# Experts in units of 64 tokens, two neighbouring units per step, each expert's weights loaded once in fixed order

## The reference

```
g_top, g_idx = lax.top_k(softmax(t @ w_grp + b_grp), 1)          # 1 of 4 groups
e_sel = the 4 logits of that group out of t @ w_rtr + b_rtr
e_top, e_idx = lax.top_k(softmax(e_sel), 2)                      # 2 of its 4 experts
expert_id = g_idx * 4 + e_idx                                    # 16 experts
weights = g_top * e_top / sum(e_top)
a = einsum('td,edf->tef', t, w_gate); u = einsum('td,edf->tef', t, w_up)   # d 1024, f 256
hid = silu(a) * u * gates
y = einsum('tef,efd->td', hid, w_down)
```

```
layer 0  pairs 314 152 100 198 7 13 11 7 89 88 30 33 85 45 55 53
         tiles   3   2   1   2 1  1  1 1  1  1  1  1  1  1  1  1   = 20
         units   5   3   2   4 1  1  1 1  2  2  1  1  2  1  1  1   = 29, 15 steps of two units
layer 1  pairs 204  88 198 114 19 34 33 54 38 34 14 42 77 152 55 124
         tiles   2   1   2   1  1  1  1  1  1  1  1  1  1   2  1   1   = 19
         units   4   2   4   2  1  1  1  1  1  1  1  1  2   3  1   2   = 28, 14 steps of two units
```

```
layer 0  0-0 0-0 0-1 1-1 2-2 3-3 3-3 4-5 6-7 8-8 9-9 10-11 12-12 13-14 15
layer 1  0-0 0-0 1-1 2-2 2-2 3-3 4-5 6-7 8-9 10-11 12-12 13-13 13-14 15-15
```

## Time and profile before

| what | value |
| --- | --- |
| median of 3 runs | 1613.76 us (1613.31 to 1620.27) |
| the profiled execution | 1615.13 us |
| its span, first to last instruction | 1613.4 us |
| mean granted TensorE clock | 0.928 |
| PE busy | 1388.2 us |
| gate/up products of L1903 | 279.9 us busy, 624 instructions |
| down products of L1926 | 140.5 us busy, 312 instructions |
| expert stage of layer 0, first gate/up to last down | 548.7 to 784.7 us |
| expert stage of layer 1 | 1333.9 to 1557.5 us |

### The profile page before, as it was taken

The page is one execution under the profiler, slowest core; times in us unless marked ns, Lnnn a source line. Parts: engine busy times, 40 slices in busy tenths (PEclk is TensorE's granted clock), DMA queues, the critical chain, the costliest instruction groups (busy, mean ns, idle before and its releaser), DMA issues.

```text
span 1613.4 us, 22451 instructions
## 1 busy us (share of the span) xinstructions
PE 1388.2 (86%) x8194; PEld 840.4 (52%) x8194; DVE 728.6 (45%) x1673; ACT 434.2 (27%) x991; POOL 245.3 (15%) x374
## 2 busy tenths in 40 slices
PE   4999978999998699999479997799999939999950
PEld 3455455777676454545144554477776724454420
DVE  0345325767544334343345442377764343343426
ACT  2111146666301011111121103466660101111112
POOL 3311020000200122111302001100011010111114
PEclk8899989999998799999789997899999959999985
DMA  9500694001305699999560034800111029999943
GB/s 333 188 12 1 246 372 102 1 1 41 118 40 183 233 356 356 386 372 359 181 224 12 1 106 168 250 2 2 40 51 42 27 82 352 367 370 368 369 161 146
DMA packets 152035, 283.17 MB, mean 176 GB/s; under 512 B 7312, under 2 KB 95632, under 8 KB 146928
## 3 DMA queue, kind: packets, MB, share of 16 engines
q1 hardware_dynamic: 126832, 197.41, 36.5%
q0 software_dynamic: 25088, 84.24, 14.0%
HBM read 244.43 MB, written 37.29 MB: 175 GB/s over the span
## 4 chain that ended last, share of the span: by engine, by line
PE 50%; DVE 8%; DMA 5%; DVEq 2%; issue 2%; ACT 1%; POOL 0%; SPq 0%; POOLq 0%; ACTq 0%
PE ps L1903 16%; PE ps L1926 7%; PE ps L1642 7%; PE ps L1540 6%; PE ps L1818 4%; PE ps L1698 3%; PE ps L1751 2%; DMA ring<-in_w_mod 2%; DMA ring<-in_moe_w_up 1%; DVE ring L1221 1%; DVE x L1059 1%; DVEq L1053 1%; PE ps L1558 1%; PE ps L1874 1%; PE ps L1840 1%
## 5 line engine op out<-in xcount | busy, mean ns | idle before, releaser
L1903 PE MATMUL ps<-ring,hT_region 128*128 128x512 f32 x624 | 279.9, 602 | 2.6 <-DVE hT_region L1482 1.7
L1642 PE MATMUL ps<-ring,hT_region 128*128 128x512 f32 (+1 forms) x640 | 270.6, 579 | 1.7 <-ACT hT_region L848 1.7
L1221 DVE TENSOR_SCALAR_CACHE_REDUCE ring<-ps 128x768 f32<-128x768 f32 (+1 forms) x168 | 132.7, 820 | 164.8 <-PE ps L1698 108.4
L1642 PEld LDWEIGHTS ps<-ring,hT_region 128*128 128x128 f32 x640 | 121.2, 193 | 133.5 <-issue 132.7
L1903 PEld LDWEIGHTS ps<-ring,hT_region 128*128 128x128 f32 x624 | 117.6, 194 | 137.9 <-issue 137.0
L907 ACT ACTIVATE ring<-ring,negm 128x768 f32<-128x768 f32 (+1 forms) x168 | 137.7, 820 | 33.3 <-DVE ring L1221 33.2
L1818 PE MATMUL ps<-ring,hT_region 128*128 128x384 f32 (+1 forms) x480 | 141.8, 453 | 0.0
L1926 PE MATMUL ps<-arena,work 128*128 128x512 f32 x312 | 140.5, 593 | 1.1 <-DVE work L1505 1.1
L1698 PE MATMUL ps<-arena,qT 64*128 64x384 f32 (+1 forms) x640 | 127.5, 517 | 13.2 <-DVE ring L1221 5.7
L1489 DVE TENSOR_SCALAR work<-work 128x256 f32<-128x256 f32 x39 | 11.5, 294 | 263.2 <-ACT work L995 263.2
L1818 PEld LDWEIGHTS ps<-ring,hT_region 128*128 128x128 f32 x480 | 89.8, 190 | 44.2 <-issue 0.7
(11 more groups left out here) (270 smaller groups left out, 1612.0 us busy)
## 6 DMA issues: line engine op xcount, KB each, us to landing
ring<-in_w_mod SPq DMA_DIRECT2D x24, 2048.0 KB, 12.1
ring<-in_moe_w_gate SPq DMA_DIRECT2D x39, 1024.0 KB, 11.9
ring<-in_moe_w_up SPq DMA_DIRECT2D x39, 1024.0 KB, 15.4
arena<-in_moe_w_down SPq DMA_DIRECT2D x39, 1024.0 KB, 7.9
y_rows<-arena POOLq DMA_DIRECT2D x39, 512.0 KB, 7.7
ring<-in_w_in SPq DMA_DIRECT2D x6, 2048.0 KB, 18.9
y_rows<-x POOLq DMA_DIRECT2D x1, 7680.0 KB, 25.9
arena<-mod_rows POOLq DMA_DIRECT2D x14, 512.0 KB, 6.2
```

The lines of the kernel that those rows point to most:

```text
L1221: ts(o_, i_, -pair_of(p)[4], None, ALU.mult, ALU.min, accum_out=col).then_inc(m_ready, 1)
L1642: last = mm(ps[:, b, 0:n], hT[:, c, t * P:(t + 1) * P], w[:, c, :], start=(c == 0), stop=(c == KC - 1))
L1903: last = mm(ps[:, 2 + i % 2, :], hgT[i % 2][:, c, :], w[:, c, :], start=(c == 0), stop=(c == KC - 1))
```

## The change

The slots of an expert are now counted in units of 64 instead of tiles of 128, with at least one unit for each expert (k64[0] is -1). A step takes two neighbouring units, 128 slots as before. If both belong to one expert, the products are as before. If they belong to two, each product is issued as two, with 64 columns of the stationary operand each: the odd expert's slots are the first half and write PSUM partitions 0 to 63, the even expert's write 64 to 127. N_ET falls from 25 to 18. The DVE works out, for each step, which form it has (EI_FORM), in which ring slot the first operand lies (EI_A), and for each unit its expert, its slot and whether its expert is new (EI_NEW); PE and SP read these into registers and branch on them. PE's operand addresses in ring and arena now come from a register.

Each expert's weights are loaded once, in the order 0 to 15, expert e into the slot LATE[e % 4], gate/up in the ring and down in four arena buffers instead of two. Experts 0 to 3 are loaded without waiting for the routing, each as its ring slot comes free, the down weights once the output projection is done. An expert from 4 on is loaded when its first unit comes up: gate/up for step i when gate_up(i - 2) is done, down for step i - 1 when down(i - 3) is done.

On PE gate_up(i) now goes ahead of hidden_T(i - 1), and on DVE the copy of the rows of tile i + 1 ahead of hidden(i). The new tables are made on DVE behind r_hot and ahead of the copy of idx; the gate weights rout_w move behind it. Some constants and buffers move, and a 256-byte table is loaded at the start.

```diff
+HALF = P // 2
+N_ET = ((N_PAIR + NE * HALF) // HALF - 1 + 1) // 2
...
+LATE = (3, 2, 0, 1)
+EVEN_SLOTS = (LATE[0], LATE[2])
...
-        uses += [("moe", l, i, late[i % RING]) for i in range(N_ET)]
+        uses += [("moe", l, e, LATE[e]) for e in range(RING)]
...
+            def gate_up_of_step(l, i):
+                sp.wait_ge(gu_done[l], i - 1)
+                for u in (2 * i, 2 * i + 1):
+                    with first_of_expert(u):
+                        e, at = expert_and_slot(l, u)
+                        gate_up_weights(l, e, ring[:, bass.ds(sp.snap(at * 4096), 4096)], wgu_landed[l][u % RING])
+                    with sp.Else():
+                        sp.sem_inc(wgu_landed[l][u % RING], 32)
+            def down_of_step(l, i):
+                sp.wait_ge(dn_done[l], i - 1)
...
                 if kind == "moe":
+                    slot_free(g)
+                    gate_up_weights(l, l * NE + i, to, wgu_first[i])
+                    if i == 0:
+                        sp.wait_ge(wo_done, l * 15 + 15)
+                    down_weights(l, l * NE + i, arena[:, DN0 + 2048 * at:DN0 + 2048 * (at + 1)], wd_first[i])
+                    if i == RING - 1:
+                        sp.wait_ge(experts_ready, l + 1)
+                        for step in range(2, N_ET + 1):
+                            if step < N_ET:
+                                gate_up_of_step(l, step)
+                            if step > 2:
+                                down_of_step(l, step - 1)
...
+                tt(r_le.rearrange("p (e s) -> p e s", e=NE), lane[:, 0:NE].unsqueeze(2).to_broadcast([P, NE, NE]),
+                   lane[:, 0:NE].unsqueeze(1).to_broadcast([P, NE, NE]), ALU.is_ge)
                 dve.wait_ge(r_count, l + 1)
...
-                tt(b6, r_incl[0:1, :].unsqueeze(1).to_broadcast([1, N_ET, NE]),
-                   iota_t[0:1, :].unsqueeze(2).to_broadcast([1, N_ET, NE]), ALU.is_le)
-                red(r_ex[0:1, :], b6, AX.X, ALU.add)
+                ts(r_par, r_incl[:, 0:NE:2], 0.5, None, ALU.mult)
+                tt(b7, r_par.unsqueeze(2).to_broadcast([P, NE // 2, N_ET + 1]),
+                   halves.unsqueeze(1).to_broadcast([P, NE // 2, N_ET + 1]), ALU.is_equal)
+                red(r_par, b7, AX.X, ALU.add)
+                tt(v3(r_add, NE), v3(r_rank, NE), r_lim.unsqueeze(1).to_broadcast([P, NT, NE]), ALU.is_ge)
...
                 last.then_inc(r_hot, 1)
+                tt(b6, r_incl[row, :].unsqueeze(1).to_broadcast([1, N_HALF, NE]),
+                   iota_t[row, :].unsqueeze(2).to_broadcast([1, N_HALF, NE]), ALU.is_le)
+                red(r_ex[row, :], b6, AX.X, ALU.add)
+                for k in range(2):
+                    dve.drain()
+                    tt(b9, b8, by_step[row, k, :].unsqueeze(1).to_broadcast([1, N_ET, 2 * NE]), ALU.mult)
+                    dve.drain()
+                    red(r_steps[row, k * N_ET:(k + 1) * N_ET], b9, AX.X, ALU.add)
+                tt(b6, b6, slot_step[row, :].unsqueeze(1).to_broadcast([1, N_HALF, NE]), ALU.mult)
+                red(r_at[row, :], b6, AX.X, ALU.add)
...
+                stt(experts_i[row, EI_NEW + 1:EI_NEW + N_HALF], r_ex[row, 1:N_HALF], float(RING), r_one[row, 1:N_HALF],
+                    ALU.is_ge, ALU.mult).then_inc(experts_ready, 1)
+                dve.wait_ge(r_rows, l + 1)
+                cp(idx[:], ps[:, 6, 352:352 + N_ET]).then_inc(idx_ready, 1)
...
                 def gate_up(i):
+                    form[i] = pe.value_load(experts_i[0:1, EI_FORM + i:EI_FORM + i + 1], min_val=0, max_val=2)
+                    a_at[i] = pe.value_load(experts_i[0:1, EI_A + i:EI_A + i + 1], min_val=0, max_val=RING - 1)
...
+                        wa = ring[:, bass.ds(pe.snap(a_at[i] * 4096), 4096)].rearrange("p (c n) -> p c n", c=KC)
+                        def of_two(b):
+                            wb = slot[b].rearrange("p (c n) -> p c n", c=KC)
+                            for c in range(KC):
+                                mm(g[0:HALF, :], h[:, c, 0:HALF], wa[:, c, :], start=(c == 0), stop=(c == KC - 1))
+                                last = mm(g[HALF:P, :], h[:, c, HALF:P], wb[:, c, :],
+                                          start=(c == 0), stop=(c == KC - 1))
+                            last.then_inc(gu_done[l], 1)
+                        with pe.If(form[i] > 1):
+                            for c in range(KC):
+                                last = mm(g, h[:, c, :], wa[:, c, :], start=(c == 0), stop=(c == KC - 1))
+                            last.then_inc(gu_done[l], 1)
+                        with pe.Else():
+                            with pe.If(form[i] > 0):
+                                of_two(EVEN_SLOTS[1])
+                            with pe.Else():
+                                of_two(EVEN_SLOTS[0])
+                    else_inc(pe, i, gu_done[l], 1, i)
...
                 for i in range(N_ET + 1):
+                    if i < N_ET:
+                        gate_up(i)
                     if i >= 1:
                         hidden_T(i - 1)
-                    if i < N_ET:
-                        gate_up(i)
```

More of the change, by code:

```diff
@@ L81, with step_tables @@
 MOD_FIRST = 4
+LATE = (3, 2, 0, 1)
+EVEN_SLOTS = (LATE[0], LATE[2])
+def step_tables():
+    at = [LATE[x % RING] for x in range(NE)] + [0]
+    a, form = [], []
+    for x in range(NE):
+        odd, even = (x, x + 1) if x % 2 else (x + 1, x)
+        a += [at[x], at[odd]]
+        form += [2, EVEN_SLOTS.index(LATE[even % RING])]
+    out = np.zeros((2, 2, NE), np.float32)
+    for k, g in enumerate((a, form)):
+        for x in range(NE - 1):
+            out[k, 1, x] = g[2 * x + 1] - g[2 * x]
+            out[k, 0, x] = g[2 * x + 2] - g[2 * x + 1]
+    return out
 def ring_uses():
-    late = (3, 2, 0, 1)
     uses = [("mod", 0, j, j) for j in range(MOD_FIRST)]
@@ L92, in ring_uses @@
         if l + 1 < DEPTH:
-            uses += [("mod", l + 1, j, late[j]) for j in range(MOD_FIRST)]
-        uses += [("moe", l, i, late[i % RING]) for i in range(N_ET)]
+            uses += [("mod", l + 1, j, LATE[j]) for j in range(MOD_FIRST)]
+        uses += [("moe", l, e, LATE[e]) for e in range(RING)]
     return uses
@@ L467, in down_weights @@
[L467 to L477 removed]
+                else:
+                    sp.wait_ge(gu_done[ul], N_ET)
@@ new lines, in down, with of_two @@
+                        h = hidT[i % 2]
+                        def of_two(b):
+                            wb = arena[:, DN0 + 2048 * b:DN0 + 2048 * (b + 1)].rearrange("p (c n) -> p c n", c=2)
+                            for k in range(2):
+                                y = ps[:, 5 + k, :]
+                                for c in range(2):
+                                    cols = slice(k * 512, (k + 1) * 512)
+                                    mm(y[0:HALF, :], h[:, c, 0:HALF], wa[:, c, cols], start=(c == 0), stop=(c == 1))
+                                    last = mm(y[HALF:P, :], h[:, c, HALF:P], wb[:, c, cols],
+                                              start=(c == 0), stop=(c == 1))
+                            last.then_inc(dn_done[l], 1)
@@ new lines, in down @@
+                        with pe.If(form[i] > 1):
+                            for k in range(2):
+                                for c in range(2):
+                                    last = mm(ps[:, 5 + k, :], h[:, c, :], wa[:, c, k * 512:(k + 1) * 512],
+                                              start=(c == 0), stop=(c == 1))
+                            last.then_inc(dn_done[l], 1)
+                        with pe.Else():
+                            with pe.If(form[i] > 0):
+                                of_two(EVEN_SLOTS[1])
+                            with pe.Else():
+                                of_two(EVEN_SLOTS[0])
```

203 lines of the change are left out of this document (118 added, 85 removed).

## The result

The changed kernel takes 1569.66 us (median of 4 runs, 1563.83 to 1573.47) against 1614.34 us (4 runs, 1613.31 to 1620.27): a ratio of 0.9713, 95% interval 0.9669 to 0.9757. That is 44.7 us less, where 63 were forecast. The profiled execution took 1566.19 us, its span is 1564.0.

A forecast was written before the change was run, and what follows sets the result against it. PE and the DMA engines were both taken to be at their limit in the expert stages. Gains 114.2 + 5.0 less 7.8, 4.5, 1.3, 3, 36.3 and 3 made 63.3 us: 1551 us, range 1518 to 1595, likeliest 1535 to 1571.

The forecast's parts named there:

- Work removed: Expert stages on PE: ten tile periods of 11.42 us go, two-expert steps costing nothing extra; 114.2 us gained.
- Late weights: Expert stages: PE waits for experts loaded after the fourth, 36.3 us over both layers, plus 3 us of lower clock afterwards.
- The lead: Late loads: PE needs a load 16.0 us after T, the end of gate/up two steps before the first load's.
- the first rival: Expert stages: weights keep up better, stalls 0 to 22 us, 1511 to 1535; against it, 75.5 MB in eight steps; chance 0.14.
- Branches, registers and shapes: PE in the expert steps: register loads, branches and changes of product shape cost 3 us in all, between 0 and 10.
- Order on PE: Start of each expert stage: gate/up of step 1 ahead of step 0's hidden transposes gains 2.5 us a layer, 5.0 together.
- Routing 7.8: Routing on DVE: longer row placing and step tables ahead of idx cost 3.9 us a layer, 7.8 us.
- gather 4.5: Layer 0's first gather meets the early loads of the first four experts and takes 4.5 us longer.
- h_rows 1.3: Layer 1: early expert loads delay the last h_rows store that DVE waits for; 1.3 us, between 0 and 4.7.
- that the halves don't overlap: Two-expert steps: the halves run one after the other, PE pays 103 us, 1614, no change; chance 0.06.
- that jumps break PE's run-ahead: Expert steps: taken jumps and uncovered register loads cost 5.3 us a step, 51 us slower, 1665; chance 0.07.
- That the weights come later still: Expert stages: SP's register loads and in-order waits delay loads, stalls about 75 us, band 1571 to 1595; chance 0.13.

## Why the prediction was right, and where it was off

The mechanism was right and the time lies in the range; the likeliest value was 18.7 us too low by the medians, 14.4 by the profiled executions. The balance goes by the latter, with spans:

- **Work removed, 114.2 us: right.** Ten periods went, and the halves of a two-expert step run at the full-width pace, as the attention's L1751 had suggested; separating them cost 5.2 us a step. By the Trainium skill ("TensorEngine Tiling (Array Packing)", Key Properties) a change of tiling mode drains the engine. The trace agrees in that each change costs a little: the first pair of halves starts 0.53 us after the last full-width product (577.35 to 577.88) and the next pair 0.48 us later, where starts lie 0.43 apart within either kind, and full-width transposes start 0.52 us after the last pair. That is 0.1 to 0.2 us a change, within the 0.2 of the prediction.
- **Late weights, 36.3 + 3 of clock: the mechanism is right, both terms mis-sized.** Taking the late loads away gave 49.0 us; by the traces, first to last gate/up fell by 25.2 and 25.6, 50.7 against 39.3. The lead was the weak step. Let T be 1365.8, the end of gate/up of step 4. By the term's own figures the first new pair lands at T + 13.9 (2 x 5.45 + 3), in time for T + 16.0; it landed at T + 20.5, and step 6 waited 4.7 us. SP issued its first late loads at 1368 and the pair's last at 1372.4. The up load of expert 12 landed at 1453.4, T + 87.6, where the term had T + 79.3; the rate was some 375 to 382 GB/s, not 385. Steps 10 and 11, by which the term measured the delay, did not wait themselves: the delay had come in steps 6, 8 and 9. And the clock: PE's window stands at 0.50 behind a wait of 4.7 us, and gate/up of that step took 9.5 us in place of 7.1. Against the same steps without late loads, gate/up of steps 6, 8 and 9 of layer 1 took 2.4, 2.5 and 3.0 us longer, and of steps 7, 11 and 13 of layer 0 2.6, 1.4 and 1.5: 13.4 in all, where I had 3 us and at most 8. With PE's idle 35.4 us that is 48.8 of the 50.7. So in the trace the larger part of the miss stands as slow products, not as idle time, though a faster product would in part have waited longer.
- **The prediction's 75.5 MB "in eight steps" is wrong.** That is the late weights of both layers; the last eight steps of one layer bring 37.7 MB. The argument against the first rival was half as strong as it read; the stalls themselves were summed with the right sizes.
- **Branches, registers and shapes, 3 us, at most 10: too small.** Without late loads the 27 step intervals take 322.1 us where 27 x 11.42 are 308.3: 13.8 us. 0.27 a one-expert step is the down product's branches behind its wait, as moving the waits shows; a two-expert step takes 12.0 to 12.5. With the waits moved a two-expert step of layer 0 still took 11.69 us against 11.43, which leaves 0.26 for its changes of shape. In the changed kernel only some 6 us of the 13.8 stand in steps that don't wait, the rest lies under waits for weights. What I called hidden in gate/up was hidden, but only by the new order: with the old one 0.9 us a step came out.
- **Order on PE, 5.0: right** (13.98 to 11.50 and 11.84, 4.6 together), **but its other side was missing.** With gate/up ahead, the last hidden transposes and both last down products stand bare at the stage's end: last gate/up to last down is 17.24 us against 15.25 in layer 1, as here (the 0.54 of the earlier trace rows is now 1.27 and more). Two us a layer, a term that I had not written down.
- **Routing 7.8, gather 4.5, h_rows 1.3: right.** From the last router product to the first gate/up it is 7.7 us more in layer 0 (8.4 forecast) and 6.8 in layer 1 (5.2); DVE waits 2.6 us for the store, the gather takes 8.00.

```profile
1492.30 6.87 PE ps L2022 x16
1499.17 0.23 PE ps L1641 x2
1499.40 1.27 issue
...
1505.83 3.71 PE ps L2067 x8
```

Stages: 25.0 us more than forecast, of which 11.4 for late weights with their clock, 9.5 for the step intervals without them and 4.1 for the tails; routing 0.9 more; and 11.8 us less elsewhere, in stretches that the change does not touch: 8.7 of them between layer 0's experts and layer 1's router, where the granted clock was higher. The first row is of the kernel before, the second of the one after, at the same place, between the input projection and attention.

```profile
974.30:994.70 20.40, 14.21 (x114) 9.11 (x112) 5.65 (x28) 6.44 (x24) 0.00 (x0) 0.67 0.01 3
```
```profile
953.00:969.80 16.80, 10.62 (x112) 6.70 (x110) 5.62 (x28) 6.11 (x23) 0.00 (x0) 0.90 0.00 1
```

25.0 + 0.9 - 11.8 = 14.1; by the spans the difference is 13.9, the rest is rounding. The stretch between layer 0's experts and layer 1's router is in part one of luck: it took 517.7 us before and 509.0 after, and in the eleven profiled executions of the experiments, which have the same work there, 507.8 to 517.3 us, at a granted clock of 0.930 to 0.952. Whether a part of the 8.7 us belongs to the change, one trace of the kernel before can't tell. So the forecast's closeness owes something to a clock that fell on its side: the terms themselves missed by 25.9 us, more than the 18.7 of the medians.

The rivals: that the halves don't overlap fell with the timeline; that jumps break PE's run-ahead fell with steps of 11.7 us. That the weights come later still, 1571 to 1595, was missed by 1.3 us only: two of the four runs, 1573.1 and 1573.5, lie in its band, and what it named, SP's register loads and waits in order, stands in the trace, though with stalls of 50.7 us and not of 75. By the Trainium skill ("Runtime: NRT & Kernel Launch", Instruction fetch mechanics) a taken branch beyond the fetched window waits for a fetch. The trace has long branches, whether fetches or not, but where nobody waits, in skipping unused steps at a stage's end (ns min/median/max):

```profile
L439 PEldq COMPARE_BRANCH  x64: 65/73/3212, 673.5 to 1522.3; - x64
```

## What to carry to other kernels

When a change takes work from an engine while the DMA engines are full, ask for each load when its buffer is really free and issue it then, not a fixed number of steps ahead; here that was worth more than half as much as the change itself. Make each wait name the data of the step at hand: a count that is merely safe can eat all of an early start. Write the end of a pipeline down as a term when an order changes, and put branches and address arithmetic ahead of the last wait before a product, not behind it.

## What the runs showed of the hardware

- Half-width products to different halves overlap only while they stand near each other in the queue: alternating 7.0 us, grouped 12.2, with four pairs side by side at the seam. There the first of the second half starts ahead of the last three of the first, which stand before it in the queue.
- A change between full-width and half-width products costs 0.1 to 0.2 us: starts 0.52 to 0.53 us apart in place of 0.43, and some 0.05 to 0.1 more at the next start.
- A 1 MB load takes SP 0.35 us (down) or 0.57 us (gate or up) to issue into free engines and up to 7.7 us into full ones (the latter with the first four loads behind the routing). SP's register loads of 0.27 and 0.15 us, three pairs for an expert, come on top of that, and all of SP's later loads queue behind.
- In the changed kernel six PE waits of 4.7 to 6.8 us are each followed by a gate/up that is 1.4 to 3.0 us longer; behind the first of layer 1 the granted clock stands at 0.50 (the level of 1.2 GHz) from 1386 to 1391. In the run without late down loads a wait of 3.7 us is followed by none of this, and the next one, of 2.0 us, by 1.7 us.
- The longest branch took 3.2 us, against 73 ns in the median.
